# Opening norm of a streaming encoder step: row scaling moved from a scaled copy into the transposing matmul

## The chip, the cores and the metric

One core of a Trainium2 chip runs the whole program. The metric is the device time of one execution in microseconds (us). An execution that the profiler records has a time of its own, which is not the median of the unprofiled runs.

## What is computed

The reference is one layer of a streaming encoder on 1,024 prompt frames and 8 x 16 sample frames, 1,152 rows of 1,024 channels in all. The part that the change touches is the first line of the layer, an RMS norm followed by the combined input projection:

```
y = xf * lax.rsqrt(jnp.mean(xf * xf, axis=-1, keepdims=True) + EPS)
h = y * g_pre_mix
z = h @ w_in          # (1152, 1024) @ (1024, 10240)
```

After it come retention and HGRN2 heads, gates, an output projection and a squared-ReLU MLP. All of them read `z`, and none of them is touched.

## The kernel before

The projections take the normalised input with channels on the partitions, so the nine tiles of 128 rows are normalised and transposed first. The tiles XH and XL hold the result as a high and a low part, each 128 x 8 x 1152. Every product of a weight block (`gemm`, L593 to L595) is then made of three passes: WHI with XH, WHI with XL, WLO with XH, each as eight matmuls of 128 x 384 for each third `c` of the rows.

The opening is a pipeline over the nine row tiles `tt`. Each engine runs its own list in the order in which it is written, and semaphores join the lists:

- SP loads the raw rows XR[tt], all nine in buffers of their own, with ident, gcol, LB and the first two weight blocks in between.
- ACT squares and sums a tile (`first_sq`, L930, n_ss), writes the scaled row tile HR (L949, n_hr), and copies the transposed tile to XH (`norm_xh`, L908, two halves). Its order in iteration `tt` is: square of tile tt+1, HR of tile tt, at tt = 2 and 5 the high part of a weight block (WHI), XH of tile tt-1.
- DVE turns the sum into mean plus EPS (`norm_ms`, L1216), POOL raises it to the power -0.5 (L1604, rsc, n_rs).
- PE transposes HR in eight 128 x 128 pieces (`norm_transpose`, L581), four to a PSUM bank, with one signal (n_tp) for each bank.
- DVE multiplies each bank with the gain into TM (`norm_cols`, L1234), and subtracts XH from TM into XL (L1239). Its order in iteration `tt` is: mean of tile tt+1, at tt = 3 and 6 the low part of a weight block (WLO, L1209), then TM and XL of tile tt-1.

The first weight block's product is cut up and put between the transposes on PE: half of its first third after tile 3, the other half after tile 4, the second third after tiles 6 and 7, and the last third when all nine tiles are ready. These pieces are called product A, B, C and D below, and the last third is called the final third. From the final third on PE has a product to do at all times.

The second use of `norm_transpose` (L856, before the MLP) has no counterpart in the change: it transposes HR2, which DVE scales in `norm_row` (L1223).

Of the kernel before, what the change touches and what calls it, by code (L numbers as in the profile page):

```python
# [12 lines left out]
F32 = mybir.dt.float32  # L13
F32R = mybir.dt.float32r
U32 = mybir.dt.uint32
ALU = mybir.AluOpType
ACT = mybir.ActivationFunctionType

P = 128
D = 1024  # L20
# [4 lines left out]
NT = T // P  # L25
# [40 lines left out]
def program(nc, a, o, scr):  # L66
    ctx = ExitStack()
    with ctx:
        def sem(name):
            return ctx.enter_context(nc.semaphore(name))  # L70

        def sb(name, shape, dt=F32, stack=ctx):
            return stack.enter_context(nc.sbuf_tensor(name, shape, dt))
# [13 lines left out]
        ident = sb("ident", [P, P])  # L87
# [7 lines left out]
        rsc = sb("rsc", [P, 2 * NT])  # L95
        dss, dms, drs = sb("dss", [P, 2 * NT]), sb("dms", [P, NT]), sb("drs", [P, NT])
        yss, yms, yrs = (sb(n, [P, NT]) for n in ("yss", "yms", "yrs"))
        psum = [ctx.enter_context(nc.psum_tensor(f"bank{i}", [P, 512], F32)) for i in range(8)]
# [4 lines left out]

        p0 = ExitStack()
        XR = [sb(f"XR{i}", [P, D], F32, p0) for i in range(NT)]
        HR = [sb(f"HR{i}", [P, D], F32, p0) for i in range(2)]
        TM = [sb(f"TM{i}", [P, 4, P], F32, p0) for i in range(2)]
        SQJ = sb("SQJ", [P, D], F32, p0)
        p0.close()
# [106 lines left out]
        n_ss, n_ms, n_rs, n_hr = sem("n_ss"), sem("n_ms"), sem("n_rs"), sem("n_hr")  # L216
        n_tp, n_tm, n_xh, n_xl = sem("n_tp"), sem("n_tm"), sem("n_xh"), sem("n_xl")
# [90 lines left out]
        def row_bank(t, q):  # L308


            return psum[((7, 3) if t == 0 else (0, 1) if t % 2 else (2, 7))[q]]
# [257 lines left out]

        @block.tensor  # L570
        def _(pe):
            def norm_transpose(tt, src):

                b = 3 + 2 * (tt % 2)
                pe.wait_ge(n_hr, tt + 1)
                for g in range(2):
                    if tt >= 2:
                        pe.wait_ge(n_tm, 2 * (tt - 2) + g + 1)
                    for i in range(4):
                        k = 4 * g + i  # L580
                        last = pe.transpose(psum[b + g][:, i * P:(i + 1) * P], src[:, k * P:(k + 1) * P], ident[:, :])  # L581
                    last.then_inc(n_tp, 1)

            def gemm(n, m, p, c, first=False, w=None, part=range(KT)):


                if c == 0:
                    pe.wait_ge(w_lo, (n if w is None else w) + 1)
                if not first:
                    pe.wait_ge(ev, NC * (n - 1) + c + 1)  # L590
                s = slice(c * CH, (c + 1) * CH)
                for k in part:
                    pe.matmul(psum[c][:, 0:CH], WHI[p][:, k, :], XH[:, k, s], start=(k == 0), stop=False)  # L593
                    pe.matmul(psum[c][:, 0:CH], WHI[p][:, k, :], XL[:, k, s], start=False, stop=False)  # L594
                    last = pe.matmul(psum[c][:, 0:CH], WLO[p][:, k, :], XH[:, k, s], start=False, stop=(k == KT - 1))  # L595
                    if k == KT - 1:
                        last.then_inc(mm, 1)
# [3 lines left out]
                pe.sem_inc(s, 1)  # L601
            pe.wait_ge(c_in, 48)
            for tt in range(NT):
                norm_transpose(tt, HR[tt % 2])
                if tt in (3, 6):
                    pe.wait_ge(n_xh, 2 * tt)
                    pe.wait_ge(n_xl, 2 * tt)
                    gemm(0, 0, 0, tt // 3 - 1, first=True, part=range(0, KT // 2))
                if tt in (4, 7):
                    gemm(0, 0, 0, tt // 3 - 1, first=True, part=range(KT // 2, KT))  # L610
# [225 lines left out]
            for t in range(NT + 2):  # L836
                if t < NT:
                    s = slice(t * P, (t + 1) * P)
                    pe.wait_ge(sp_hi, 6 * KT + KT * (t // TPC + 1))
                    pe.wait_ge(sp_lo, 6 * KT + KT * (t // TPC + 1))  # L840
                    if t == 1:
                        pe.wait_ge(ev, NC * NB1 - 1)
                    if t == 2:
                        pe.wait_ge(ev, NC * NB1)
                    if t >= 2:
                        pe.wait_ge(d_x1, t - 1)
                    for q in range(2):
                        bank = row_bank(t, q)
                        ns = slice(512 * q, 512 * (q + 1))
                        for k in range(KT):  # L850
                            pe.matmul(bank[:, :], XH[:, k, s], WOH[:, k, ns], start=(k == 0), stop=False)  # L851
                            pe.matmul(bank[:, :], XH[:, k, s], WOL[:, k, ns], start=False, stop=False)  # L852
                            last = pe.matmul(bank[:, :], XL[:, k, s], WOH[:, k, ns], start=False, stop=(k == KT - 1))  # L853
                    last.then_inc(d_mm, 1)
                if t >= 2:
                    norm_transpose(NT + t - 2, HR2[(NT + t - 2) % 2])  # L856
                if t in (NT - 1, NT):
                    c = t - NT + 1
                    pe.wait_ge(n_xh, 2 * NT + 2 * TPC * (c + 1))
                    pe.wait_ge(n_xl, 2 * NT + 2 * TPC * (c + 1))  # L860
                    pe.wait_ge(d_x1, NT - 1)
                    pe.wait_ge(w_lo, W_FFN + 1)
                    up(0, 0, c)
# [40 lines left out]
        def _(act):  # L904
# [12 lines left out]
            def whi_block(n, m, p, free=True):  # L917
                whi(n, p, m, as_block(WRAW[p]), WHI[p][:, :, :], 3 * n - 3 if free else None)
# [13 lines left out]
            def norm_xh(tt, tm, t):  # L932
                for g in range(2):
                    act.wait_ge(n_tm, 2 * tt + g + 1)
                    copy(XH[:, 4 * g:4 * g + 4, t * P:(t + 1) * P], tm[g][:, :, :]).then_inc(n_xh, 1)

            def first_sq(tt):
                act.wait_ge(x_in[tt], 16)
                norm_sq(tt, XR[tt], SQJ)

            first_sq(0)
            for tt in range(NT + 1):
                if tt < NT - 1:
                    first_sq(tt + 1)
                if tt < NT:
                    act.wait_ge(n_rs, tt + 1)
                    if tt >= 2:
                        act.wait_ge(n_tp, 2 * (tt - 2) + 2)
                    act.activation(HR[tt % 2][:, :], XR[tt][:, :], ACT.Copy, scale=rsc[:, tt:tt + 1]).then_inc(n_hr, 1)  # L949
                if tt == 2:  # L950
                    whi_block(0, 0, 0, free=False)
                if tt == 5:
                    whi_block(1, 0, 1, free=False)
                if tt:
                    norm_xh(tt - 1, TM, tt - 1)
# [178 lines left out]
            for t in range(NT + 2):  # L1134
                if t < NT:
# [4 lines left out]
                    for q in range(2):  # L1140
                        last = act.activation(SQJ2[:, 512 * q:512 * (q + 1)], row_bank(t, q)[:, :], ACT.Square,
                                              accum_out=dss[:, 2 * t + q:2 * t + q + 1])
# [60 lines left out]
        def _(dve):  # L1203
# [7 lines left out]
            def wlo_block(n, p):  # L1211
                wlo(n, as_block(WRAW[p]), WHI[p][:, :, :], WLO[p][:, :, :])

            def norm_ms(tt):
                dve.wait_ge(n_ss, tt + 1)
                dve.tensor_scalar(msc[:, tt:tt + 1], ssc[:, tt:tt + 1], 1.0 / D, EPS, ALU.mult, ALU.add).then_inc(n_ms, 1)  # L1216
# [8 lines left out]
            def norm_cols(tt, tm, which, t):  # L1225

                b = 3 + 2 * (tt % 2)
                for g in range(2):
                    dve.wait_ge(n_tp, 2 * tt + g + 1)
                    if tt:  # L1230
                        dve.wait_ge(n_xh, 2 * (tt - 1) + g + 1)
                        dve.wait_ge(n_xl, 2 * (tt - 1) + g + 1)
                    gain = gcol[:, which, 4 * g:4 * g + 4].unsqueeze(2).to_broadcast([P, 4, P])
                    dve.tensor_tensor(tm[g][:, :, :], psum[b + g][:, :].rearrange("p (k t) -> p k t", k=4),  # L1234
                                      gain, ALU.mult).then_inc(n_tm, 1)
                for g in range(2):
                    dve.wait_ge(n_xh, 2 * tt + g + 1)
                    ks, ts = slice(4 * g, 4 * g + 4), slice(t * P, (t + 1) * P)
                    dve.tensor_tensor(XL[:, ks, ts], tm[g][:, :, :], plain(XH[:, ks, ts]), ALU.subtract).then_inc(n_xl, 1)  # L1239
# [6 lines left out]
                              ALU.subtract).then_inc(lb_ch, 1)  # L1246
            norm_ms(0)
            for tt in range(NT + 1):
                if tt < NT - 1:
                    norm_ms(tt + 1)  # L1250
                if tt == 3:
                    wlo_block(0, 0)
                if tt == 6:
                    wlo_block(1, 1)
                if tt:
                    norm_cols(tt - 1, TM, 0, tt - 1)
# [259 lines left out]
            for t in range(NT + 2):  # L1516
# [13 lines left out]
                if 1 <= t <= NT:  # L1530
                    tt = NT + t - 1
# [259 lines left out]
```

## Time and profile before

| | us |
|---|---|
| median of 3 runs | 2538.49 (2537.8 to 2539.58) |
| profiled execution | 2545.82 |
| its span | 2544.0 |
| PE busy in the span | 2479.0 (97%) |
| start of the final third on PE | 44.64 |

The span runs from the first to the last recorded instruction; 1.82 us of the profiled execution's time lie around it. A busy PE row counts overlapping matmuls once. PE's loads of its stationary operand (PEld) run beside its matmuls, so the distance between two starts, and not the duration of one, is what a matmul costs in a row of them.

### The profile page before, as it was taken

How to read it: one execution, taken by the hardware profiler on the slowest of the kernel's cores; microseconds unless marked ns; L12 is line 12 of the kernel's file. 1: busy time of each engine (PE TensorE's matmuls, PEld its weight loads, DVE VectorE, ACT ScalarE, POOL GpSimd, SP SyncE). 2: the span in 40 equal slices, each digit the busy share in tenths (PEclk: the TensorE clock that was granted, in tenths of full speed). 3: DMA queues.
4: the chain of work that ended last, by engine and by line, in shares of the span. 5: the costliest groups of instructions: out<-in, count | busy, mean ns of one | idle time of the engine just before them, and what ended most of it. 6: DMA issues, size and time to landing. Idle time of an engine off the chain costs nothing.

```text
span 2544.0 us, 37470 instructions
## 1 busy us (share of the span) xinstructions
PE 2479.0 (97%) x14264; PEld 2358.0 (93%) x14264; DVE 1157.3 (45%) x2297; ACT 674.2 (27%) x1365; POOL 491.4 (19%) x729
## 2 busy tenths in 40 slices
PE   6999999999999999999999999999999999999998
PEld 6999999999999999999999999988899898898996
DVE  4053424324276666566657435555343343333335
ACT  5222232323222222222222323333121131131221
POOL 1021211102164455445436000001000000000000
PEclk8999999999999999999999999999999999999999
DMA  4251625343333313313323633222021021110114
GB/s 150 90 191 64 225 81 196 103 166 117 121 102 124 117 66 132 123 65 119 127 88 113 216 125 130 93 99 85 17 67 39 27 66 33 33 58 25 50 41 157
DMA packets 219182, 256.88 MB, mean 101 GB/s; under 512 B 8256, under 2 KB 186816, under 8 KB 218944
## 3 DMA queue, kind: packets, MB, share of 16 engines
q1 hardware_dynamic: 219072, 255.37, 30.4%
q8 instruction: 74, 1.21, 0.2%
q14 instruction: 36, 0.29, 0.0%
HBM read 175.12 MB, written 80.22 MB: 100 GB/s over the span
## 4 chain that ended last, share of the span: by engine, by line
PE 72%; issue 12%; DVE 11%; DMA 2%; POOL 2%; ACT 1%; SPq 0%; DVEq 0%; POOLq 0%; ACTq 0%
PE bank L593 10%; PE bank L595 10%; PE bank L594 10%; PE bank L823 5%; PE bank L825 5%; PE bank L824 5%; PE bank L893 5%; PE bank L892 5%; PE bank L894 5%; PE bank L744 3%; DVE QE L1374 2%; DVE PP L1377 2%; PE bank L851 1%; PE bank L853 1%; PE bank L852 1%
## 5 line engine op out<-in xcount | busy, mean ns | idle before, releaser
L593 PE MATMUL bank<-XH,WHI 128*128 128x384 f32 x2304 | 792.9, 344 | 14.3 <-DVE WLO L1209 5.5
L595 PE MATMUL bank<-XH,WLO 128*128 128x384 f32 x2304 | 775.8, 337 | 0.0
L594 PE MATMUL bank<-XL,WHI 128*128 128x384 f32 x2304 | 775.6, 337 | 0.0
L593 PEld LDWEIGHTS bank<-XH,WHI 128*128 128x128 f32 x2304 | 437.6, 190 | 20.4 <-ACT ZST L908 7.1
L594 PEld LDWEIGHTS bank<-XL,WHI 128*128 128x128 f32 x2304 | 437.5, 190 | 0.9
L595 PEld LDWEIGHTS bank<-XH,WLO 128*128 128x128 f32 x2304 | 436.6, 190 | 0.0
L908 ACT ACTIVATE ZST<-bank 128x384 f32<-128x384 f32 x240 | 117.9, 492 | 575.4 <-PE bank L595 573.7
L823 PE MATMUL bank<-XH,WHI 128*128 128x384 f32 x768 | 257.7, 335 | 3.6 <-ACT XH L908 3.6
L825 PE MATMUL bank<-XH,WLO 128*128 128x384 f32 x768 | 257.2, 335 | 0.0
L824 PE MATMUL bank<-XL,WHI 128*128 128x384 f32 x768 | 257.2, 335 | 0.0
L1209 DVE TENSOR_TENSOR WLO<-WRAW,WHI 128x1024 fp32r<-128x1024 f32 x128 | 157.4, 1230 | 210.7 <-ACT WHI L908 205.5
L893 PE MATMUL bank<-WDL,UH 128*128 128x512 f32 x576 | 224.1, 389 | 0.0
L894 PE MATMUL bank<-WDH,UL 128*128 128x512 f32 x576 | 224.1, 389 | 0.0
L892 PE MATMUL bank<-WDH,UH 128*128 128x512 f32 x576 | 224.1, 389 | 0.0
L1586 DVE TENSOR_TENSOR ACC<-ACC,bank 128x512 f32<-128x512 f32 x144 | 98.9, 687 | 247.5 <-PE bank L894 247.5
L1604 POOL TENSOR_TENSOR ORS<-OMS,mhalf 128x1 f32<-128x1 f32 x108 | 78.2, 724 | 543.4 <-DVE OMS L1274 543.4
L1604 POOL TENSOR_TENSOR yrs<-yms,mhalf 128x1 f32<-128x1 f32 x9 | 4.9, 548 | 776.9 <-DVE yms L1546 776.9
L823 PEld LDWEIGHTS bank<-XH,WHI 128*128 128x128 f32 x768 | 144.6, 188 | 4.3 <-ACT XH L908 3.8
L908 ACT ACTIVATE WHI<-WRAW 128x1024 fp32r<-128x1024 f32 x128 | 134.7, 1052 | 42.3 <-PE bank L595 40.8
L824 PEld LDWEIGHTS bank<-XL,WHI 128*128 128x128 f32 x768 | 144.7, 188 | 0.3
L825 PEld LDWEIGHTS bank<-XH,WLO 128*128 128x128 f32 x768 | 144.7, 188 | 0.0
L894 PEld LDWEIGHTS bank<-WDH,UL 128*128 128x128 f32 x576 | 108.1, 188 | 22.5
(173 smaller groups left out, 3231.0 us busy)
## 6 DMA issues: line engine op xcount, KB each, us to landing
scratch_z<-ZST SPq DMA_DIRECT2D x80, 576.0 KB, 2.8
WRAW<-in_w_in SPq DMA_DIRECT2D x80, 512.0 KB, 3.8
HZ<-scratch_z SPq DMA_DIRECT2D x32, 576.0 KB, 5.2
WRAW<-in_w_up SPq DMA_DIRECT2D x32, 512.0 KB, 4.1
WRAW<-in_w_down SPq DMA_DIRECT2D x32, 512.0 KB, 3.3
MG<-scratch_z SPq DMA_DIRECT2D x16, 576.0 KB, 5.9
ZQ<-scratch_z SPq DMA_DIRECT2D x4, 1152.0 KB, 5.5
ZK<-scratch_z SPq DMA_DIRECT2D x4, 1152.0 KB, 7.8
```

Source lines behind the costliest of these rows:

```text
L593: pe.matmul(psum[c][:, 0:CH], WHI[p][:, k, :], XH[:, k, s], start=(k == 0), stop=False)
L594: pe.matmul(psum[c][:, 0:CH], WHI[p][:, k, :], XL[:, k, s], start=False, stop=False)
L595: last = pe.matmul(psum[c][:, 0:CH], WLO[p][:, k, :], XH[:, k, s], start=False, stop=(k == KT - 1))
L823: pe.matmul(psum[c][:, 0:CH], WHI[b % 2][:, k, :], XH[:, k, s], start=(k == 0), stop=False)
L824: pe.matmul(psum[c][:, 0:CH], WHI[b % 2][:, k, :], XL[:, k, s], start=False, stop=False)
L825: last = pe.matmul(psum[c][:, 0:CH], WLO[b % 2][:, k, :], XH[:, k, s], start=False, stop=(k == KT - 1))
L892: pe.matmul(bank[:, :], UH[:, k, s], WDH[:, k, ns], start=(k == 0), stop=False)
L893: pe.matmul(bank[:, :], UH[:, k, s], WDL[:, k, ns], start=False, stop=False)
L894: last = pe.matmul(bank[:, :], UL[:, k, s], WDH[:, k, ns], start=False, stop=(k == 3))
L908: return act.activation(dst, src, ACT.Copy)
L1209: dve.tensor_tensor(lo, src, plain(hi), ALU.subtract).then_inc(w_lo, 1)
L1586: dve.tensor_tensor(ACC[:, t, ns], ACC[:, t, ns], psum[3 + x % 5][:, :], ALU.add).then_inc(dn_ev, 1)
```

## The change

HR is gone. Instead DVE multiplies ident with the inverse norms of a tile's rows, which gives a 128 x 128 diagonal DGR (two buffers). PE then takes the raw tile XR as stationary operand and this diagonal as moving operand, in an ordinary F32 matmul and no longer in a transpose: the result is the transposed and scaled piece. The scaled copy leaves ACT's list; the diagonal enters DVE's list at the head of each iteration, ahead of the next tile's mean.

```diff
-        HR = [sb(f"HR{i}", [P, D], F32, p0) for i in range(2)]
+        DGR = [sb(f"DGR{i}", [P, P], F32, p0) for i in range(2)]
...
-            def norm_transpose(tt, src):
+            def norm_transpose(tt, src, diag=None):
...
-                        last = pe.transpose(psum[b + g][:, i * P:(i + 1) * P], src[:, k * P:(k + 1) * P], ident[:, :])
+                        out, rows = psum[b + g][:, i * P:(i + 1) * P], src[:, k * P:(k + 1) * P]
+                        if diag is None:
+                            last = pe.transpose(out, rows, ident[:, :])
+                        else:
+                            last = pe.matmul(out, rows, diag[:, :], start=True, stop=True, skip_group_check=True)
...
-                norm_transpose(tt, HR[tt % 2])
+                norm_transpose(tt, XR[tt], DGR[tt % 2])
...
-                if tt < NT:
-                    act.wait_ge(n_rs, tt + 1)
-                    if tt >= 2:
-                        act.wait_ge(n_tp, 2 * (tt - 2) + 2)
-                    act.activation(HR[tt % 2][:, :], XR[tt][:, :], ACT.Copy, scale=rsc[:, tt:tt + 1]).then_inc(n_hr, 1)
...
             norm_ms(0)
             for tt in range(NT + 1):
+                if tt < NT:
+                    dve.wait_ge(n_rs, tt + 1)
+                    if tt >= 2:
+                        dve.wait_ge(n_tp, 2 * (tt - 2) + 2)
+                    dve.tensor_scalar(DGR[tt % 2][:, :], ident[:, :], rsc[:, tt:tt + 1], None, ALU.mult).then_inc(n_hr, 1)
                 if tt < NT - 1:
                     norm_ms(tt + 1)
```

## Rows read from the trace of the kernel before

**Rows 1.** The page: busy engines, and PE's busy tenths in 40 slices.

```profile
PE 2479.0 (97%) x14264; PEld 2358.0 (93%) x14264; DVE 1157.3 (45%) x2297; ACT 674.2 (27%) x1365; POOL 491.4 (19%) x729
PE   6999999999999999999999999999999999999998
```

**Rows 2.** Stretches of the opening: PE, PEld, DVE, ACT, POOL busy us (instructions), clock, DMA share, GB/s.

```profile
8.80:12.20 3.40, 3.35 (x16) 2.95 (x16) 2.17 (x5) 3.18 (x6) 0.55 (x1) 1.00 1.08 374
15.50:18.30 2.80, 0.00 (x0) 0.00 (x0) 2.33 (x4) 2.77 (x5) 0.80 (x1) 0.50 0.95 380
21.20:24.90 3.70, 3.66 (x12) 3.69 (x13) 2.84 (x6) 3.70 (x8) 0.60 (x2) 0.50 0.00 0
26.20:28.30 2.10, 2.10 (x15) 2.10 (x14) 2.00 (x4) 1.86 (x4) 0.00 (x0) 1.00 0.00 0
31.10:33.10 2.00, 0.17 (x2) 0.00 (x0) 1.79 (x3) 2.00 (x3) 0.00 (x0) 0.85 0.00 0
33.10:36.80 3.70, 3.66 (x12) 3.69 (x12) 2.69 (x5) 3.34 (x6) 0.55 (x1) 0.50 0.03 7
38.60:41.00 2.40, 2.40 (x14) 2.40 (x13) 2.13 (x4) 1.26 (x2) 0.00 (x0) 0.85 0.00 0
```

**Rows 3.** The chain that ended last, its pieces in the opening (start us, us, what).

```profile
7.50 1.16 ACT HR L949
8.80 1.95 PE bank L581 x8
10.77 0.70 DVE TM L1234
...
13.17 1.04 ACT HR L949
...
25.41 0.65 PE bank L581 x4
...
37.32 1.71 PE bank L581 x8
...
41.34 0.45 PE bank L581 x4
```

**Rows 4.** The timeline, ACT and DVE: tile 1's TM and XH, then one ordinary tile.

```profile
13.31 1.29 DVE L1234 TENSOR_TENSOR TM<-bank,gcol 128x512 f32<-128x512 f32 x2
...
15.06 1.13 ACT L908 ACTIVATE XH<-TM 128x512 fp32r<-128x512 f32 x2
...
21.36 1.13 ACT L949 ACTIVATE HR<-XR,rsc 128x1024 f32<-128x1024 f32 x1
21.48 0.15 DVE L1216 TENSOR_SCALAR msc<-ssc 128x1 f32<-128x1 f32 x1 [0.35 <-ACT SQJ L930]
21.59 1.29 DVE L1234 TENSOR_TENSOR TM<-bank,gcol 128x512 f32<-128x512 f32 x2
22.39 1.15 ACT L908 ACTIVATE XH<-TM 128x512 fp32r<-128x512 f32 x2
...
23.45 1.04 ACT L930 ACTIVATE SQJ<-XR 128x1024 f32<-128x1024 f32 x1
```

**Rows 5.** The timeline of PE: eight transposes of a tile, at different clocks.

```profile
14.26 1.09 PE L581 MATMUL bank<-ident,HR 128*128 128x128 f32 x8 [1.79 <-ACT HR L949]
18.32 1.97 PE L581 MATMUL bank<-ident,HR 128*128 128x128 f32 x8 [2.97 <-ACT HR L949]
```

**Rows 6.** PE in a retention tile: L635 is two transposes, L638 and L639 one F32 matmul each.

```profile
315.66 0.38 PE L635 MATMUL bank<-ident,KR 128*128 128x128 f32 x2
315.88 0.39 PE L638 MATMUL bank<-QR,KR 128*128 128x128 f32 x2
316.11 0.39 PE L639 MATMUL bank<-QR,KR 128*128 128x128 f32 x2
```

**Rows 7.** DVE multiplying by a column of scalars, groups by form (busy us, mean ns).

```profile
L1223 DVE TENSOR_SCALAR HR<-X1R,rsc 128x1024 f32<-128x1024 f32 x9 | 6.8, 753 | 6.0 <-POOL rsc L1604 6.0
L1216 DVE TENSOR_SCALAR msc<-ssc 128x1 f32<-128x1 f32 x9 | 1.3, 148 | 0.3 <-ACT SQJ L1151 0.3
```

## The prediction

> **What bounds the kernel now.** I read the page first. PE is busy for 2479.0 of 2544.0 us, and its row of tenths shows one slice below 9 at the front [rows 1]: after the opening PE has no idle time that a faster ACT or DVE could fill. So the change can act in one place only, on the moment at which the final third starts (44.64 us). Whatever that start gains or loses is carried unchanged to the end, and nothing in the change touches later code.
>
> Next I cut the opening into stretches [rows 2]. PE idles there in gaps (15.5 to 18.3 us, 31.1 to 33.1 us), and its work runs at two levels: at granted clock 0.50 (1.2 GHz) a product of 12 matmuls takes 3.7 us, at 1.00 (2.4 GHz) it takes 2.1 us. So the opening has two currencies, what waits for what, and at which clock PE works.
>
> Then the chain that ended last [rows 3]. The reader should see that the scaled copy HR is on it twice only, for tile 0 at 7.50 us and for tile 2 at 13.17 us, although it runs nine times. Transposes are on it four times: both banks of tiles 0 and 7, the first bank of tiles 4 and 8. The timeline of an ordinary tile says why the other copies cost nothing [rows 4]: HR starts at 21.36 us, and while it runs DVE makes the mean (21.48) and starts TM (21.59). Without HR, XH's second half could not start before TM ends at 21.59 + 1.29 = 22.88, and with half of XH's 1.15 us behind it ACT would take the next square at about 23.45 us, where it takes it now. The copy lies beside DVE's TM.
>
> **What is removed.** Nine ACT copies of 1.13 us, about 10 us of ACT work. By the chain two count: tile 0 (1.16 us) and tile 2 (1.04 us). The other seven are covered by TM. No DMA moves, and SP's list is unchanged. POOL's list is too.
>
> **What is added on DVE.** Nine multiplications of 128 x 128. The trace has the same operation at 1024 columns for 0.753 us and at one column for 0.148 us [rows 7]. Between them 128 columns come to 0.15 + 127/1023 x 0.60 = 0.22 us. The bounds are 0.15 and 0.75. It waits for rsc, and behind it in DVE's list stand the next tile's mean, WLO, TM and XL. For tile 0 that wait is real: it ends at 7.46 us, so the mean of tile 1 slips by some 0.6 us, which PE's work on tile 0 covers. From tile 2 on rsc was made an iteration earlier, and the diagonal falls into the time in which ACT squares (DVE waited 0.35 us for that square before 21.48). So I price it at 0.22 us once, for tile 0, and at nothing after; without that cover it would be 0.16 a tile, 1.3 us in all, and 0.7 a tile at the upper bound.
>
> **What is changed on PE.** This is the disputed part. The transposes L635 leave one record each, the F32 matmuls L638 and L639 two each: 0.22 us pass from two transposes to the next line, and 0.23 us from one matmul to the next [rows 6]. So an ordinary F32 matmul of 128 columns costs 0.22 us at full clock where a transpose costs 0.11. At half clock a transpose costs (1.97 - 0.48) / 7 = 0.21 us [rows 5], taking the last one's own 0.48 us off, and by doubling a diagonal matmul costs 0.43 (my estimate). A tile's eight pieces rise from 0.86 to 1.73 us, or from 1.7 to 3.4. The lower bound is 0.11, no extra at all; the upper one 0.43 throughout.
>
> **The sum, in order of time.**
> - Tile 0: HR 1.15 becomes a diagonal of 0.22, -0.93. Its eight pieces are on the chain at 0.21 extra each, +1.70. TM's second half starts 0.77 later, at 11.54, and so does the square of tile 3.
> - Tile 2: its HR goes, -1.04, leaving -0.27 for XH of tile 1 (15.06 now). But TM of tile 1 (13.31 now [rows 4]) moves 0.77 with the square of tile 3 and ends at 14.08 + 1.29 = 15.37, and XH's second half waits for it: it starts at 15.42, where it now starts half of 1.13 us behind 15.06, at about 15.6. The square of tile 4 gains 0.16 us. WLO, TM and XL of tile 2 hang on it, and product A starts at 21.05. Tile 3's pieces (16.9 to 20.3 at half clock) are done before.
> - Product A as before. Tile 4's pieces come right behind it. Half clock lasts into the first two of them: the first bank is late by 0.5 us, the second by 0.8, and TM's second half now waits for it. Through XH, the square of tile 7, WLO and TM, product C starts -0.16 + 0.8 = 0.65 late, at 33.76. Tiles 5 and 6 (3.5 us at full clock, behind product B at 28.95) end at 32.4, inside PE's old gap.
> - From product C to the end of product D PE alone sets the pace, and the clock decides. As before the change, product C at half clock (3.7 us) and tile 7 at half clock: +1.6. With product C at full clock and tile 7 at half: -1.6 + 1.6 = 0. With both at full clock, tile 7 costs -0.1, product C -1.6 and product D -0.3 (2.4 to 2.1), together -2.0.
> - Tile 8: first bank +0.43, and TM's second half waits 0.25 more for the second bank: +0.68.
>
> The totals are 0.65 + 0.68 = 1.33 plus 1.6, 0 or -2.0: +2.9, +1.3 or -0.7 us. I take the middle. Before, the clock was at 0.50 in product C after PE had been idle from 31.1 to 33.1 us. Now tiles 5 and 6 run back to back, and that gap shrinks to some 1.4 us, which speaks for a later fall; against it, tile 7 would then still meet half clock. On the profiled execution this gives 2545.82 + 1.3 = 2547.1 us. That execution is 7.3 us above the median of the runs, so I add the difference to the median: 2538.49 + 1.3 = 2539.8 us.
>
> The bank of tile 0 also bears on a rule. Through 8.80 to 12.20 us PE did nothing but 16 transposes, the first at half-clock distances (eight of the chain's took 1.95 us [rows 3]), and the next tile's eight took 1.09 us against 1.97 [rows 5]: the clock rose after transposes alone. The Trainium skill (TensorE: Matmul & The Clock Gate, Part 4, PE-mode transpose) says that transposes do not count as PE work for the clock in the way matmuls do. By that rule this change, which turns all 72 into matmuls, would lift the clock earlier and lead to the full-clock rival below; by the trace the transposes count already, and only their greater length helps.
>
> **The rivals.**
> - *The clock stays full.* Longer pieces leave PE fewer gaps, and the half-clock stretches of product A, C, D and the one at 46.2 us vanish. Product A gives -1.6, the three totals' lowest case -0.7, and a stretch of 3.4 us at half clock in the final third another 3.4 x (1 - 2.1/3.7) = -1.5: -3.8 us, 2534.7. Against it: the gap of 2.8 us before 18.3 hardly shrinks, because PE waits there for rows and not for its own work.
> - *Half clock throughout, the one on the slower side.* PE then becomes the bound from product A on: four products of 3.7 and five tiles of 3.4 make 31.8 us, from 21.05 to 52.9, plus the 2.6 us from tile 8's last piece (about 42.0: product D ends at 41.0, and eight pieces take 1.0) to the final third: 55.5 against 44.64, +10.9 us, 2549.4. It decides once some 5 us of this is met, about half of that work. Against it: PE worked without a pause from 21.2 us and had full clock at 26.2 [rows 2]; more work makes no more pauses.
> - *A diagonal matmul costs no more than a transpose.* Then the two copies on the chain are pure gain: -0.93 - 1.04 = -1.9 us, 2536.6. Against it: the two records of each F32 matmul [rows 6].
> - *The diagonal delays DVE's list* (0.75 us each, or uncovered): +1.3 to +3 us on top, 2541 to 2543. Against it: DVE's wait for the square in every tile.
>
> **How the numbers follow.** The runs before span 1.8 us; I take 0.2%, 5.1 us, as what this measurement tells from no change. I give the three totals 0.72 together (the middle one most), the full clock 0.08, half clock throughout 0.04, the cheap matmul 0.05, the late DVE list 0.11. Only half clock throughout lies beyond 5.1 us by itself. Of the full clock and the cheap matmul 0.03 is for both at once (-3.8 - 1.9 = -5.7), and of the late DVE list 0.03 for its upper bound on top of the +2.9 case (+5.9). That makes 0.03 faster, 0.90 within 0.2%, and 0.04 + 0.03 = 0.07 slower. The range runs from the cheap matmul or the -0.7 case with scatter, 2536.3, to the +2.9 case with a partly late DVE list, 2543.0. It leaves out the two clock rivals and the tails.
>
> **What would show it.** L581 should leave 144 records in the opening instead of 72, at distances of 0.11 us (full clock) or 0.21 (half). PE's first one should come near 7.8 us instead of 8.80, TM's second half near 11.5, product A near 21.1, product C near 33.8, and the final third within -0.7 to +2.9 us of 44.64. ACT should show idle time in front of XH where HR stood. The diagonal should take about 0.22 us and DVE should still wait for squares. The prediction is wrong if the granted clock in product A is 1.00, if tiles 4 and 5 run at 0.50, or if PE has new gaps after 50 us.

## The result, and the profile after

The changed kernel takes 2553.68 us (median of 6 runs, 2550.98 to 2560.79), the kernel before 2539.03 us beside it (6 runs, 2537.28 to 2543.37). The ratio is 1.0062 with a 95% interval from 1.0052 to 1.0072: slower by 13 to 18 us. I had forecast 2539.8 us, within 0.2% of before.

The page of the changed kernel first: span, busy engines, and the queue that fetches instructions. The line of that queue in the kernel before was one that I had not read; it said 74 packets and 1.21 MB.

```profile
span 2551.4 us, 37614 instructions
PE 2485.9 (97%) x14336; PEld 2366.5 (93%) x14336; DVE 1160.9 (46%) x2306; ACT 665.0 (26%) x1356; POOL 491.9 (19%) x729
q8 instruction: 102, 1.67, 0.3%
```

Against [rows 1] PE is busy for 6.9 us more in a span that is 7.4 us longer, with 72 matmuls and 72 loads more. The profiled execution of before, 2545.82 us, lies 6.8 us above the median of its runs and that of the changed kernel does not, so the two spans differ by less than the medians.

The opening, which is all that the prediction spoke of, in the timeline of the changed kernel: PE's pieces (L585 here, answering to [rows 5]), the start of product A and of the final third, and a diagonal.

```profile
7.61 0.28 DVE L1252 TENSOR_SCALAR DGR<-ident,rsc 128x128 f32<-128x128 f32 x1 [0.74 <-POOL rsc L1608]
8.04 8.17 PE L585 MATMUL bank<-DGR,XR 128*128 128x128 f32 x48 [8.04 <-DVE DGR L1252]
...
17.30 2.05 PE L585 MATMUL bank<-DGR,XR 128*128 128x128 f32 x16 [1.08 <-DVE DGR L1252]
...
21.37 0.41 PE L597 MATMUL bank<-XH,WHI 128*128 128x384 f32 x1 [2.02 <-ACT XH L912]
...
31.97 0.41 PE L597 MATMUL bank<-XH,WHI 128*128 128x384 f32 x1 [0.83 <-DVE XL L1238]
...
42.22 0.41 PE L597 MATMUL bank<-XH,WHI 128*128 128x384 f32 x1 [2.27 <-DVE XL L1238]
```

Product A starts at 21.37 us, product C at 31.97 and the final third at 42.22, where it was 44.64: the opening is 2.4 us shorter, not longer. The stretches that answer to [rows 2] (same columns) show the clock at 1.00 in both products, where it was 0.50:

```profile
21.30:23.40 2.10, 2.03 (x12) 2.06 (x13) 1.85 (x5) 1.24 (x4) 0.55 (x1) 1.00 0.03 8
32.00:34.00 2.00, 2.00 (x12) 2.00 (x13) 1.75 (x5) 1.13 (x4) 0.55 (x1) 1.00 0.01 4
```

So the time is lost elsewhere. The list of PE's waits, longest first in total (us, times, longest), has in second place a line that stood at 1.1 us in two waits before the change:

```profile
PE bank L597 <- issue: 10.5, 4, 3.6
```

"issue" says that nothing which the profile shows held PE up. Three of the four stand in the timeline at the same point of the retention loop (`pe.Fori(0, RH)`, four iterations), where the branch goes back to the first product of the next iteration. Between them stands the line of L669, which both kernels reach once an iteration.

```profile
241.04 1.97 PE L669 MATMUL bank<-ZK,QXB 128*128 128x256 f32 x8 [0.61 <-DVE UB L1288]
279.93 0.68 PE L597 MATMUL bank<-XH,WHI 128*128 128x384 f32 x1 [3.18 <-issue]
384.67 1.97 PE L669 MATMUL bank<-ZK,QXB 128*128 128x256 f32 x8 [0.61 <-DVE UB L1288]
423.59 0.68 PE L597 MATMUL bank<-XH,WHI 128*128 128x384 f32 x1 [3.20 <-issue]
...
567.45 0.44 PE L597 MATMUL bank<-XH,WHI 128*128 128x384 f32 x1 [3.56 <-issue]
```

From one L669 to the next pass 143.6 us. The same line of the kernel before:

```profile
241.06 1.97 PE L665 MATMUL bank<-ZK,QXB 128*128 128x256 f32 x8 [0.61 <-DVE UB L1284]
...
379.91 1.97 PE L665 MATMUL bank<-ZK,QXB 128*128 128x256 f32 x8 [0.61 <-DVE UB L1284]
```

That is 138.85 us, so this iteration has become 4.8 us longer. 3.2 us are the gap; the rest is the clock behind it, less a wait of some 1.1 us that falls away: before, PE waits once an iteration for the low part of a weight block, and in the three iterations behind a gap the changed kernel doesn't.

```profile
302.84 0.43 PE L593 MATMUL bank<-XH,WHI 128*128 128x384 f32 x1 [1.09 <-DVE WLO L1209]
```

Two stretches of the changed kernel (columns of [rows 2]), the gap and what follows:

```profile
276.70:280.00 3.30, 0.12 (x2) 0.07 (x1) 0.29 (x1) 2.83 (x3) 0.00 (x0) 0.86 0.70 252
280.00:283.30 3.30, 3.30 (x11) 3.30 (x12) 0.94 (x1) 0.00 (x0) 0.00 (x0) 0.50 0.49 120
```

The first stretch in the kernel before:

```profile
276.70:280.00 3.30, 3.30 (x21) 3.30 (x20) 0.25 (x1) 2.84 (x3) 0.00 (x0) 1.00 0.75 272
```

After the gap PE makes 11 matmuls in 3.3 us at 0.50, before the change 21 at 1.00. The three gaps do not cost the same. From L669 to L669 the changed kernel takes 143.63, 143.51 and 141.40 us; behind the third gap (567.45 us) the clock stays at 1.00, and that iteration is only 2.6 us longer than the 138.8 us of an undisturbed one (the gap of 3.6 us less the wait of some 1 us). And the instruction queue, asked for 300 to 700 us (three iterations), first in the changed kernel, then in the kernel before:

```profile
q8 instruction: 24, 0.39, 0.4%
```

```profile
q8 instruction: 1, 0.02, 0.0%
```

Before the change PE runs through the retention loop again and again and next to nothing is fetched; now nine packets of 16 KB come in each iteration (9 from 277 to 420 us, 9 from 420 to 563.9 us). One of them falls into the gap itself, from 276.7 to 279.9 us:

```profile
q8 instruction: 1, 0.02, 2.0%
```

It starts between 277 and 278 us, right behind PE's last matmul; the gaps at 420.4 and 563.9 us have one each as well, and the kernel before has none from 276.7 to 279.9 us. PE's code in this loop is the same, instruction for instruction. What the change did to it is to shift it: 72 pieces now leave two records each instead of one, a load and a matmul more, 144 instructions in front of the loop.

### The profile page after: what moved, and what is told of

Its sections match the earlier page's. It is cut to its first block, busy times and chain, and to the rows that moved or that the text cites. A ratio compares the mean times of both kernels' runs of the same rounds, so it can differ in the third digit from the quotient of the medians.

```text
span 2551.4 us, 37614 instructions
## 1 busy us (share of the span) xinstructions
PE 2485.9 (97%) x14336; PEld 2366.5 (93%) x14336; DVE 1160.9 (46%) x2306; ACT 665.0 (26%) x1356; POOL 491.9 (19%) x729
## 4 chain that ended last, share of the span: by engine, by line
PE 74%; issue 12%; DVE 9%; POOL 2%; ACT 1%; DMA 1%; SPq 0%; DVEq 0%; POOLq 0%; ACTq 0%
PE bank L597 11%; PE bank L599 11%; PE bank L598 11%; PE bank L827 5%; PE bank L828 5%; PE bank L829 5%; PE bank L896 5%; PE bank L898 5%; PE bank L897 5%; PE bank L748 3%; DVE QE L1378 2%; DVE PP L1381 2%; PE bank L857 1%; PE bank L855 1%; PE bank L856 1%
```

## The experiments

Theory A: the time is lost because the retention loop lies elsewhere in PE's code, so that it no longer fits into what PE keeps of its instructions and has to be fetched anew. Theory B: it is the diagonal matmuls, by their length or by the clock. Each can be had without the other: the position without the matmuls, and the matmuls without the position.

For every kernel I read three numbers: the start of the final third on PE (the opening), the time from there to the first transpose of the HGRN2 loop (the four retention iterations and what lies before them), and the instruction packets from 300 to 700 us.

| kernel | final third, us | from there to HGRN2, us | packets | time, us | ratio to before, 95% |
|---|---|---|---|---|---|
| before | 44.64 | 671.4 | 1 | 2539.03 | |
| changed | 42.22 | 683.4 | 24 | 2553.68 | 1.0052 to 1.0072 |
| e1 before, 144 increments | 57.95 | 680.5 | 24 | 2568.19 | 1.0096 to 1.0127 |
| e2 before, 112 increments | 50.87 | 681.3 | 23 | 2562.59 | 1.007 to 1.0096 |
| e3 changed, 112 increments | 54.12 | 666.9 | 0 | 2547.31 | 1.0019 to 1.0044 |
| e4 changed, transposes of raw rows | 41.87 | 669.1 | 1 | 2537.41 | 0.9976 to 0.9998 |
| e5 before, loop at slot 160 | 44.35 | 682.5 | 24 | 2555.56 | 1.005 to 1.0082 |
| e6 changed, loop at slot 16 | 42.17 | 668.7 | 1 | 2537.26 | 0.9981 to 1.0002 |
| e7 changed, branch hint | 43.89 | 668.5 | 1 | 2544.33 | 1.0 to 1.0027 |
| e8 scaled copy and F32 matmul, slot 16 | 44.94 | 668.4 | 1 | 2540.0 | 0.9996 to 1.0014 |
| e9 before, loop at slot 130 | 44.76 | 679.6 | 24 | 2548.82 | 1.0026 to 1.005 |
| e10 e6 with hint in HGRN2 loop | 42.26 | 668.2 | 1 | 2537.75 | 0.9985 to 1.0009 |
| e11 before, loop at slot 64 | 43.67 | 668.1 | 1 | 2536.65 | 0.9989 to 1.0012 |

The medians of before in the four batches were 2539.59, 2538.52, 2538.22 and 2538.48 us, the single runs scattering from 2531.94 to 2547.53. The third column is the steady one: 666.9 to 671.4 in one group, 679.6 to 683.4 in the other, and nothing between; the packets divide the kernels in the same way. What lies behind it, from the first transpose of the HGRN2 loop to the end of the span, does not: 1820.9 to 1834.1 us in the five kernels of the second group and 1820.5 to 1832.7 us in the eight of the first.

**e1 and e2, instructions in front, norm untouched.**

```diff
+            for _ in range(144):          # e2: 112
+                pe.sem_inc(pe_pad, 1)
             pe.wait_ge(c_in, 48)
```

> The kernel before, norm untouched, with 144 semaphore increments that nobody waits for ahead of PE's first wait. The change adds 72 pieces with one record more each, a load and a matmul, which makes PE's code longer by 144 instructions as well. Theory A (position of PE's code): the slowdown comes from where the retention loop lies in PE's code and not from the norm. Then this kernel is slower than before by 14 to 18 us (the retention loop takes 143.6 us an iteration instead of 138.8, and there are no 2.4 us won in the opening), PE has gaps of about 3.2 us near 280, 424 and 567 us, and the instruction queue moves about 100 packets instead of 74. Theory B (the longer diagonal matmuls, or what they do to the clock, cost the time): no retention loop slows down, within 1.5 us of before.

> The same with 112 increments instead of 144. Theory A, with the loop's end just over an edge of a code block in the changed kernel (its last instruction packet is fetched at 278.77 us, one us before the loop starts again): 32 instructions less keep the loop on one block less, so this kernel takes the time of before within 1.5 us, with 74 packets. If what costs is only the number of instructions, and no edge, it is slower by 112/144 of what 144 cost, some 12 us. Theory B: as before.

e1 shows gaps of 3.26, 3.04 and 3.58 us at the branch back, as said, and 24 packets. But it is 28.6 us slower, not 14 to 18: the increments are not free. PE reaches its first transpose at 23.23 us,

```profile
23.23 1.09 PE L582 MATMUL bank<-ident,HR 128*128 128x128 f32 x4 [23.23 <-issue]
```

instead of 8.80, some 0.16 us for each of the 144, and the final third starts 13.3 us late. Without these 13.3 us, 15.3 are left, with an untouched norm. e2 missed: I expected the loop to be safe with 112, and it is as slow (681.3 us, 23 packets). So either my idea of an edge or my place for it was wrong, and e3, e9 and e11 decide which. The time that I gave there for the last instruction packet, 278.77 us, was misread: on the clock of the profile there is none from 278 to 279 us, and the packets near the branch come between 277 and 278 and between 280 and 281 us.

**e3, the changed kernel shifted by one whole block.** The 112 increments of e2, in the changed kernel.

> The changed kernel with 112 increments ahead of PE's first wait, so that all later PE code moves by 144 + 112 = 256 instructions in all, which is 16384 bytes at 64 bytes each, the size of one instruction packet in the trace. Theory A: the retention loop lies on the blocks as before, no gaps of 3.2 us, 75 packets, and what is left is the opening's gain: 1.5 to 3 us faster than before, about 2536.5 us. Theory B: 2553 us as without the increments.

The retention part is back at 666.9 us with more instructions in front than in any of the slow kernels, 256 beyond before. A loss that grew with the number of instructions would be at its largest here. What repeats is the position within 16384 bytes. The total, 2547.31 us, is 7.7 us above before since the increments hold up the opening by 11.9 us (54.12 against 42.22); the 1.5 to 3 us of gain that I expected for the total left this out.

**e4, transposes in place of the diagonal matmuls.** The rows stay unscaled: the norm's scaling is left out of the output.

```diff
-                norm_transpose(tt, XR[tt], DGR[tt % 2])
+                norm_transpose(tt, XR[tt])
```

> The changed kernel with plain transposes of the raw rows; the diagonal is still made, but no matmul reads it, so the rows stay unscaled (the norm's scaling is left out). PE's code is as long as before. Theory A: no gaps in the retention loop, and 2 to 4 us faster than before. Theory B with the long matmuls as cause: the same. Beside the kernel with 112 increments it tells what the longer pieces cost or bring in the opening itself: I expect the two within 1.5 us.

2.2 us faster than before (the interval runs from 0.5 to 6.1 us), one packet, and the final third at 41.87 us. It fits both theories as to the loss, and serves for the opening, below.

**e5 and e6, the loop placed by hand.** The loop's first instruction is put at a given slot (of 256) of its code block, with nothing executed but one branch in front.

```diff
-            with pe.Fori(0, RH) as h:
+            with nc.Fori(0, RH, engines=[pe.engine], head_slot={pe.engine: 160}) as h:   # e6: 16, in the changed kernel
```

> The kernel before with one thing changed: the first instruction of the retention loop on PE is placed at instruction 160 of its 256-instruction code block; the increments of the earlier runs, which held PE up by 0.16 us each, are gone. Theory A (position of the loop decides): I count 6.5 blocks for the loop's body, so from 160 on it touches eight blocks and at its end the first one has been given up. Slower than before by 13 to 19 us, 2553 to 2558 us, 100 to 102 instruction packets, gaps of about 3.2 us where the loop starts again, and a final third that starts at 44.6 us as before. Rival (the increments themselves, and in the changed kernel the diagonal matmuls, cost the time): within 2 us of before.

> The changed kernel with the retention loop's first instruction at slot 16 of a block, so that the body touches seven blocks. Theory A: the 14 us are gone and what the change itself does is seen alone: the opening's 2.4 us, 2536 to 2538 us with 74 or 75 packets, final third at 42.2 us. Rival (diagonal matmuls cost the time): 2553 us.

These two settle it. e5 has the old norm, the old opening (44.35 us) and one instruction more in its count than before, and it is 17.0 us slower (interval 12.7 to 20.8), with the gaps of the changed kernel:

```profile
282.80 0.44 PE L593 MATMUL bank<-XH,WHI 128*128 128x384 f32 x1 [3.31 <-issue]
...
424.40 0.46 PE L593 MATMUL bank<-XH,WHI 128*128 128x384 f32 x1 [3.48 <-issue]
...
567.23 0.44 PE L593 MATMUL bank<-XH,WHI 128*128 128x384 f32 x1 [3.52 <-issue]
```

e6 has the whole change with all 144 diagonal records and takes 2537.26 us. Its stretch from 280 to 700 us, and below it the same of the changed kernel:

```profile
280.00:700.00 420.00, 414.14 (x2445) 398.26 (x2444) 159.35 (x264) 117.73 (x250) 74.55 (x69) 1.00 0.42 143
```

```profile
280.00:700.00 420.00, 410.86 (x2395) 395.14 (x2396) 155.19 (x258) 114.16 (x245) 72.22 (x65) 0.98 0.40 135
```

50 matmuls more fit into the same 420 us. Theory B is gone as to the loss: the diagonal matmuls are all there, and it is not.

**e7, a hint for the branch.**

```diff
-            with pe.Fori(0, RH) as h:
+            with nc.Fori(0, RH, engines=[pe.engine], hint_back_edge=True) as h:
```

> The changed kernel, its loop where it was, with a prefetch hint for the loop's backward branch at the top of each iteration on PE. Theory A says that the 3.2 us gap is the fetch of the loop's first block on demand, so a hint should hide three gaps of 3.2 us and the fall of the clock behind them, and leave the extra packets: 2539 to 2543 us, about 100 packets. If the stall were of another kind (the branch itself, or a wait), the hint would change nothing: 2553 us.

The three gaps are gone, and so are the packets, which I had not expected: one packet from 300 to 700 us. The hint adds instructions of its own (37618 records against 37614) and may have changed the loop's length or place, so it does not isolate the waiting for the branch's target from the fetching of the rest. If it left the place alone, it would also say that the loop is not too long for what PE keeps; but the place has moved a little (under e9), so that stays open. In its profile the retention part is as fast as any (668.5 us). The time, 2544.33 us, lies just above the 2539 to 2543 us expected; the 12 runs scatter from 2533.69 to 2550.36 us. The profiled execution, 7.1 us longer than that of e6, shows the difference elsewhere: 1.7 us in the opening (43.89 against 42.17, see e8) and 5.6 us behind the start of the HGRN2 loop, where two waits of PE for ATT take 5.24 and 5.40 us and e6 has 2.19 and 2.86. Why they are longer no run here shows.

**e8, half of the change.** ACT makes HR as before, PE multiplies it with ident in an ordinary F32 matmul.

```diff
-                        last = pe.transpose(psum[b + g][:, i * P:(i + 1) * P], src[:, k * P:(k + 1) * P], ident[:, :])
+                        out, rows = psum[b + g][:, i * P:(i + 1) * P], src[:, k * P:(k + 1) * P]
+                        if tt >= NT:
+                            last = pe.transpose(out, rows, ident[:, :])
+                        else:
+                            last = pe.matmul(out, rows, ident[:, :], start=True, stop=True, skip_group_check=True)
```

> Half of the change: ACT still makes the scaled copy HR, but PE multiplies it with ident in an ordinary F32 matmul instead of transposing it; the retention loop is at slot 16. It tells the two halves of the opening apart. If the 2.4 us that the changed opening gained come from the longer pieces keeping PE's clock up, they stay here too: final third near 42 to 43 us, 2537 us. If they come from the copies leaving the path, this kernel loses them and pays the longer pieces: final third at 46 to 47 us, 2541 to 2542 us.

The final third starts at 44.94 us, between my two cases, and so does the time, 2540.0 us. With e4 and e6 this gives the opening in two factors, if the clock is watched. With transposes, taking the copies off brings 44.64 to 41.87 us, -2.8, at about the same granted clock (mean over the first 45 us 0.81 before, 0.82 in e4). With matmuls it brings 44.94 to 42.17, -2.8 again, but there the clock differs (0.96 in e8, 0.98 in e6): e8 has 0.61 from 20 to 24 us, e6 1.00. The longer pieces cost 0.3 us in both comparisons (44.64 to 44.94, 41.87 to 42.17), and the second comparison has the clock on their side, 0.82 in e4 and 0.98 in e6. The clocks are the last number but two of each line:

```profile
0.00:45.00 45.00, 27.28 (x131) 25.68 (x132) 29.39 (x62) 24.88 (x42) 7.08 (x14) 0.82 0.42 147
```

```profile
0.00:45.00 45.00, 30.78 (x204) 29.95 (x205) 29.66 (x62) 24.87 (x42) 7.08 (x14) 0.98 0.42 144
```

One profile each, though, and the same opening is not the same in every execution: before, e5, e9 and e11 start their final third at 44.64, 44.35, 44.76 and 43.67 us; the changed kernel, e6, e10 and e7, which have the same opening too, at 42.22, 42.17, 42.26 and 43.89. In e7 the clock fell in product A:

```profile
21.30:23.60 2.30, 2.13 (x9) 2.16 (x10) 2.06 (x6) 1.43 (x4) 0.55 (x1) 0.73 0.04 7
```

Against e7, which has lost clock as e8 has, the copies are worth 1.1 us and not 2.8; against e11 in place of before, e4 gives 1.8. So one profile each shows that taking the copies off helps, by 1 to 3 us, and can't tell what the longer pieces cost: 0.3 us where the clock stays full, 2.0 us from e4 to e7.

**e9 and e11, the edge.** Slots 130 and 64 in the kernel before.

> The kernel before with the retention loop's first instruction at slot 130 of its block, where slot 160 was slow. I count 1652 instructions for the body, 6.45 blocks: from slot 130 it ends at 6.96 blocks, inside the seventh. If the number of blocks touched decides and my count is right, this is as fast as before (within 2 us, 75 packets, no 3.2 us gaps) with 30 instructions less than the slow one. If the slowdown grows with the slot instead of having an edge, it lies between, some 12 to 14 us slower. If the body is longer than I count, it is slow as from slot 160.

> The kernel before with the retention loop's first instruction at slot 64. Slots 130 and 160 were slow, and slot 16 (in the changed kernel) was fast. If the position matters by an edge, this is either as fast as before (within 2 us, one instruction packet or so between 300 and 700 us) or as slow as slot 130 (10 to 14 us slower, 24 packets there), and nothing between. I expect fast: with 6.5 blocks counted and half a block of error in the count, the edge lies between 64 and 130.

Slot 130 is slow (679.6 us, 24 packets), slot 64 is fast (668.1 us, one). By my count of 1652 instructions slot 130 should have been safe. There is an edge, as e11 and the two separate groups of the table show, and it lies between 64 and 130, earlier than I had worked out. The packets say where the loops lie that nobody placed. The first instruction packet after 100 us comes the sooner the later the slot: reckoned from the start of the final third, at 109.3 us in e11 (slot 64), 102.6 in e9 (130) and 98.1 in e5 (160). Before has it at 111.2 us, e2 at 102.1, e1 and the changed kernel at 96.8, e7 at 94.9. So the loop of before lies ahead of slot 64, that of e2 near 130, beyond the edge, and that of the changed kernel beyond 160 and that of e7 a little further still, at a slot that no run tested without the hint; this explains e2. (Slot 16, in e6, has its first such packet at 91.5 us and its second at 112.8; only the second fits this order.)

**e10, a version to beat both.** e6 with the hint in the HGRN2 loop.

> A version that might beat both: the changed kernel with the retention loop at slot 16, and a prefetch hint for the backward branch of the HGRN2 loop, whose body is 9.5 blocks by my count and is fetched anew in each iteration wherever it lies. Before, PE has gaps of 1.2, 0.5 and 1.3 us where that loop starts again. Theory A: the hint takes up to 3 us off, 2534 to 2537 us, against 2537.3 us without it. Rival: those gaps are ACT's waits and not fetches, and nothing changes.

In the profile the gaps at that loop's branch are gone (e6 has 1.20, 0.54 and 0.81 us there) and its span is 2532.1 us, but the runs give 2537.75 us and a ratio of 0.9985 to 1.0009 to before: the 3 us that I hoped for are not in them. Such gaps decide little here: e11 has "issue" gaps of 1.81, 1.45 and 1.70 us near that branch and is no slower. No version that computes the whole layer is measurably faster than before.

## Why the prediction was wrong

**The step that failed** is the sentence in the first paragraph that "nothing in the change touches later code", and with it that what the final third gains or loses "is carried unchanged to the end". The source of the later code is untouched; its place is not, and that costs 12 to 15 us. I had read off myself that an F32 matmul leaves two records where a transpose leaves one [rows 6], and turned that into 0.11 us a piece, but not into 144 instructions ahead of every PE loop. None of the rivals was this mechanism. The one on the slower side (half clock throughout, 2549.4 us) was wrong in place and sign: the clock rose.

What it costs, by the traces: from the start of the final third to the HGRN2 loop the changed kernel needs 683.4 us, its twin with the loop at slot 16 668.7. That is 14.7 us. 11.8 of them are the three iterations that begin with a gap (143.63, 143.51 and 141.40 us against 138.83, 139.05 and 138.82), 0.4 lie behind the last L669, and 2.5 come before any branch back, ahead of the first L669: there PE waits 1.90 us for WLO (162.43 us), e6 0.95, and the clock falls behind it (0.83 from 160 to 170 us against 1.00). Of the other four kernels with packets in the loop e5 has this wait too (2.50 us) and e1 in part (1.66), e2 and e9 don't (1.06 and 1.15), so it is not shown to belong to the loop's place. The kernel before has a stray one as well, of 2.42 us at 581.71 us: that iteration takes 141.74 us, and for it the 671.4 us of before stand above the 668.1 of e11. Against the 14.7 us stand 2.4 us won in the opening: +12.3. The runs say 13 to 18 us. The remainder of a few us was not found in any trace.

The Trainium skill (Runtime: NRT & Kernel Launch, Instruction fetch mechanics) has the rule that I should have weighed: it gives PE a store of 128 KiB for instructions, refilled in blocks of 16 KiB or 256 instructions, and says that a taken branch whose target isn't in the current window of two such blocks "forces a DMA fetch of the target page before execution can continue". Taken at its word it fails here: the loop is some 6.5 blocks long (my estimate, from the code), so that its head is outside such a window at every branch back, and yet the kernel before goes back three times with one packet and without a gap. By the page's 128 KiB eight blocks fit, and the loop touches seven or eight, depending on where it begins (an estimate). The runs agree with the block (packets of 16 KB; 144 instructions harm, 256 don't), and in the slow kernels with the fetch at the branch (a packet in each gap). They show that the limit comes earlier than eight blocks by my count: from slot 130 on the loop should end within its seventh block and is already slow. Whether my count is short, one block is given up to fetching ahead, or the head is lost for another reason stays open; the nine packets an iteration are more than the loop is long, and e7 runs without them. So that the loop's place decides is shown, by e3, e5, e6, e9 and e11; that it is a matter of room is argued.

**The opening, step by step.**

- Only two of nine copies count: right in kind. The sum had -1.97 for the two, less what TM's wait gives back; the profiles give -1.1 to -2.8 us for taking them off (e4, e8), depending on which execution is compared, so the size is neither confirmed nor refuted.
- The diagonal: 0.28 us a piece, I had 0.22. It delays nothing that counts, as said; ACT waits 13.1 us in all for TM in the first 45 us, 7.1 before.
- A diagonal matmul at twice the transpose: right. Tile 3's sixteen records take 2.05 us at full clock, where eight transposes took 1.09.
- Product A at 21.37 us against 21.05 forecast: right. Behind it the sum goes wrong: products A and C ran at full clock, the case "the clock stays full", to which I gave 0.08. It was held against it that PE waits for rows before 18.3 us; but tile 3's pieces came at 17.30 us and not at 18.32, and PE's idle time ahead of them shrank from 2.97 us to 1.08. I had worked out myself that this tile would start at 16.9 us and did not carry that over into the gap. It is no certainty either: in e7, with the same opening, product A saw a fall of the clock and the final third starts 1.7 us later.
- Product C at 31.97 us, forecast 33.76; the final third at 42.22, forecast 45.9 (+1.3), outside the -0.7 to +2.9 that I gave.
- The rule on transposes and the clock (the Trainium skill, TensorE: Matmul & The Clock Gate, Part 4, PE-mode transpose): not decided anew. e4 has nothing but transposes there and a mean of 0.82, e6 matmuls and 0.98, but the matmuls are also twice as long. It can be their length or their kind. What I had read against the rule, that the clock rose through 16 transposes, rests on their distances alone: the clock column of [rows 2] reads 1.00 for that stretch from its start, although eight transposes took 1.95 us there.

What would have shown the prediction wrong stood in it: the granted clock at 1.00 in product A, and "if PE has new gaps after 50 us". Both came.

## What to carry to other kernels

Count what a change adds or removes in instructions ahead of a hardware loop, engine by engine, and look at the line of the instruction queue in the profile: a big loop that runs with next to no packets can owe that to its position, and 144 instructions in front of it can cost five to six times what the change brings in its own place (12.2 to 14.7 against 2.4 us). If a measured effect stands where nothing was edited, put the loop at a fixed place in its block in both kernels before judging the change. Here the change alone is worth nothing that can be measured on the whole (0.9981 to 1.0002), though its opening is 2.4 us shorter in most profiles.

## What was unexpected

- An "issue" gap of 3.0 to 3.7 us at each branch back of a loop that is fetched anew, and in some iterations the granted clock at 0.50 behind it (11 matmuls in 3.3 us, not 21). With it an iteration of the changed kernel is 4.5 to 4.8 us longer than in e6, without it 2.6, since a wait of some 1 us for WLO falls away.
- A semaphore increment on PE that nobody waits for takes 0.15 to 0.16 us (112 end near 18.4 us, 144 near 23.2).
- In the changed kernel, e6 and e10 the longer F32 pieces cost the opening next to nothing (0.3 us from e4 to e6, for 72 x 0.11 us of work): PE's clock was granted at 1.00 from tile 2's pieces to the end of product D, and not at 0.50 in products A and C. In e7 it was not. The stretch in the changed kernel:

```profile
14.00:43.00 29.00, 22.76 (x167) 21.96 (x166) 25.70 (x51) 18.07 (x33) 5.12 (x6) 1.00 0.15 57
```
